# Attention's longer steps: two groups of key transpositions ahead of the scores, the column-tiled products ahead of the transpositions of probabilities

## What is computed

```python
q, k, v = att_qkv(rmsnorm(yp, norm_mix[l]), w_in_att[i], q_norm_g[i], k_norm_g[i])   # prompt, 16 heads of 64
res = [dilated_band(q, k, v, d, w // d) for (w, d) in PATTERNS]       # scores, exp, weighted sum of v
o = combine_patterns([r[0] for r in res], [r[1] for r in res])
...
kall = jnp.concatenate([cache_k[i].astype(jnp.float32), kn], axis=1)  # samples: 2048 cached keys each
vall = jnp.concatenate([cache_v[i].astype(jnp.float32), vn], axis=1)
res = [dilated_gather(qs, kall, vall, d, w // d) for (w, d) in PATTERNS]
```

## Time and profile before

| what | value |
|---|---|
| median of 3 runs | 2765.56 us (2764.55 to 2767.07) |
| time of the profiled execution | 2767.65 us |
| its span | 2765.8 us, 1.85 us less than its time |
| TensorE (PE) busy | 2714.1 us, 98% |
| VectorE (DVE) busy | 1741.2 us, 63% |
| ScalarE (ACT) busy | 947.4 us, 34% |
| attention | about 1497.5 to 1910 us from the span's start |

### The profile page before, as it was taken

The page is one execution under the profiler, slowest core; times in us unless marked ns, Lnnn a source line. Parts: engine busy times, 40 slices in busy tenths (PEclk is TensorE's granted clock), DMA queues, the critical chain, the costliest instruction groups (busy, mean ns, idle before and its releaser), DMA issues.

```text
span 2765.8 us, 56498 instructions
## 1 busy us (share of the span) xinstructions
PE 2714.1 (98%) x24481; PEld 2606.5 (94%) x24481; DVE 1741.2 (63%) x2867; ACT 947.4 (34%) x1697; POOL 97.4 (4%) x220
## 2 busy tenths in 40 slices
PE   7999999999999999999999999999999999999998
PEld 7998999999999999999998777777999999999998
DVE  5754536777677777765612666657377677766676
ACT  5543523322222222432224555554232222222222
POOL 1010000000000000000011111100000000000000
PEclk9999999999999999999999999999999999999999
DMA  5120120011111111133356777863101111111112
GB/s 201 36 81 14 61 102 31 31 48 61 47 47 46 47 47 46 60 129 95 95 177 218 252 254 240 273 224 130 58 16 47 46 47 47 47 47 47 58 50 81
DMA packets 126388, 254.64 MB, mean 92 GB/s; under 512 B 7617, under 2 KB 88725, under 8 KB 125632
## 3 DMA queue, kind: packets, MB, share of 16 engines
q1 hardware_dynamic: 112944, 189.26, 20.9%
q0 software_dynamic: 11888, 57.25, 6.0%
q10 hardware_dynamic: 1312, 4.52, 0.5%
HBM read 222.98 MB, written 28.02 MB: 91 GB/s over the span
## 4 chain that ended last, share of the span: by engine, by line
PE 92%; DVE 4%; ACT 2%; DMA 1%; issue 1%; POOL 0%; SPq 0%; ACTq 0%; DVEq 0%; POOLq 0%
PE psum L1574 30%; PE psum L1629 18%; PE psum L483 14%; PE psum L224 11%; PE psum L1549 3%; PE psum L2536 2%; PE psum L2492 2%; PE psum L2452 2%; PE psum L2477 2%; PE psum L2505 1%; PE psum L2557 1%; DVE att_scores L2710 1%; PE psum L592 1%; PE psum L2481 1%; ACT smp_kt L2592 0%
## 5 line engine op out<-in xcount | busy, mean ns | idle before, releaser
L1810 DVE TENSOR_TENSOR x_res<-x_res,psum 128x544 f32<-128x544 f32 x352 | 250.4, 719 | 154.8 <-PE psum L1629 154.6
L483 PE MATMUL psum<-w_hi,h_hi 128*128 128x256 f32 x1096 | 311.5, 284 | 1.0 <-ACT qkv_tok L2092 1.0
L483 PE MATMUL psum<-w_hi,h_lo 128*128 128x256 f32 x1096 | 307.9, 281 | 0.0
L483 PE MATMUL psum<-w_lo,h_hi 128*128 128x256 f32 x1096 | 307.3, 280 | 0.0
L1629 PE MATMUL psum<-ffn_hi,ffn_unit_hi 128*128 128x272 f32 x1408 | 292.6, 289 | 1.8 <-DVE x_res L1810 1.6
L1629 PE MATMUL psum<-ffn_lo,ffn_unit_hi 128*128 128x272 f32 x1408 | 291.5, 288 | 0.0
L1629 PE MATMUL psum<-ffn_hi,ffn_unit_lo 128*128 128x272 f32 x1408 | 290.7, 288 | 0.0
L1574 PE MATMUL psum<-h_hi,ffn_unit_lo 128*128 128x272 f32 x1280 | 265.2, 288 | 0.0
L1574 PE MATMUL psum<-h_lo,ffn_unit_hi 128*128 128x272 f32 x1280 | 264.8, 288 | 0.0
L1574 PE MATMUL psum<-h_hi,ffn_unit_hi 128*128 128x272 f32 x1280 | 264.5, 288 | 0.0
L1629 PEld LDWEIGHTS psum<-ffn_hi,ffn_unit_hi 128*128 128x128 f32 x1408 | 220.7, 188 | 3.2 <-DVE x_res L1810 3.2
(11 more groups left out here) (394 smaller groups left out, 5316.7 us busy)
## 6 DMA issues: line engine op xcount, KB each, us to landing
cache_tile<-in_cache_k SPq DMA_DIRECT2D x64, 512.0 KB, 8.0
cache_tile<-in_cache_v SPq DMA_DIRECT2D x64, 512.0 KB, 13.0
w_raw<-in_w_ffn_gate SPq DMA_DIRECT2D x22, 1024.0 KB, 5.1
w_raw<-in_w_ffn_up SPq DMA_DIRECT2D x22, 1024.0 KB, 5.1
w_raw<-in_w_ffn_down SPq DMA_DIRECT2D x22, 1024.0 KB, 4.8
w_raw<-in_w_in_att SPq DMA_DIRECT2D x12, 1024.0 KB, 7.1
w_raw<-in_w_in_rec SPq DMA_DIRECT2D x10, 1024.0 KB, 4.9
park_x<-x_res POOLq DMA_DIRECT2D x2, 4368.0 KB, 13.3
```

What stands on the lines that cost most here:

```text
L483: mm = pe.matmul(PS[0:n, bank, 0:BW], st[:, k, w:w + n], mv[slot][:, k * BW:(k + 1) * BW], start=(k == 0 and x == 0) if used is None else ...
L1810: dve.tensor_tensor(x, x, pset(dset(g, i)), ALU.add).then_inc(s_res, 1)
```

## The change

In a long step (`keys_lead`) PE runs key groups 0 and 1, then the scores, then key groups 2 and 3, then at the end of phase 2 the weighted values and the sample products, and only then the turns of probabilities. ScalarE copies all four key groups before the first exponential, and VectorE takes the sample products before the probabilities' copies. The banks of the turns, their count, all shapes and all waits' values stay. Steps other than the 28 keep their order.

```diff
-    SCORED = {(0, 3): (0, 1), (1, 3): (2, 3), (2, 3): (4, 5), (3, 3): (6, 7), (4, 3): (8, 9)}
-    PV_AT = {0: 3, 1: 3, 2: 3, 3: 3, 4: 3}
+    def keys_lead(n):
+
+        return 0 <= n < NSLOT and n % QT >= 4 and sample_slot(n)[1] in (1, 2, 3, 4)
+
+    def scored(n, f):
+
+        s = sample_slot(n)[1]
+        return (2 * s, 2 * s + 1) if s is not None and s < 5 and f == (2 if keys_lead(n) else 3) else ()
+
+    def weighed_at(n):
+
+        s = sample_slot(n)[1]
+        return 1 if s is None or s > 4 else 2 if keys_lead(n) else 3
...
             b, s = sample_slot(n)
-            if 0 <= n < NSLOT and f == 1:
+            if 0 <= n < NSLOT and f == 1 and not keys_lead(n):
                 scores(n)
             for i in phase(n, f):
                 turn(n, i)
-            if 2 <= n and f == PV_AT.get(s, 1):
+            if f == 1 and keys_lead(n):
+                scores(n)
+            if 2 <= n and f == weighed_at(n):
                 pv(n - 2)
-            for t in SCORED.get((s, f), ()):
+            for t in scored(n, f):
                 tile_scores(b, t)
...
             mine = [i for i, u in enumerate(turns(n)) if by_act(u)]
-            for i in mine[0:2]:
+            first = 4 if keys_lead(n) else 2
+            for i in mine[0:first]:
                 take_act(act, n, i)
             if 0 <= n < NSLOT:
                 probs(n, 0)
-            for i in mine[2:4]:
+            for i in mine[first:4]:
                 take_act(act, n, i)
...
-                for t in SCORED.get((s, f), ()):
+                for t in scored(n, f):
                     if t % 2:
                         piece(b, t // 2)
```

## The result

The changed kernel is slower by about 3 us: 2768.52 us in the median of 22 runs (2764.97 to 2776.26) against 2765.53 (2763.81 to 2768.33, 22 runs), a ratio of 1.0012 with a 95% interval of 1.0006 to 1.0017.

What follows compares the result with a forecast made beforehand. The prediction took TensorE, 92% of 2765.8 us, as the bound; 17.1 us saved less 2.4 for shape changes and 14.6 for new VectorE waits left 0.1 us, so 2765.5 us, range 2760 to 2773.

Steps and rivals of the forecast that it cites:

- What it saves: In long steps, third and fourth key groups' delay behind ScalarE and block 7's wait for the reduction go: 17.1 us.
- Changes of shape: Blocks 4 to 7 gain a net two array-shape changes a pair of heads, at 0.17 us each: 2.4 us added.
- rival 2: The new shape change from key turns to scores costs 0.41 us in all 28 long steps: 2772.2 us, chance 0.07.
- The run of turns: New waits on VectorE's copies: 0.90 in block 6, 0.95 in block 7, 0.23 in block 0; 14.6 us added.
- Rival 1: VectorE empties the banks in time, so the 14.6 us of new waits are absent: 2750.9 us, chance 0.13.
- ScalarE: Copying all four key groups before its exponentials, ScalarE still serves the sample products in time, 0.35 us to spare.
- rival 3: ScalarE falls behind, and third key group or sample products wait again: up to 2780.6 us, chance 0.06.
- Key tiles: The key group behind the scores is asked for about 1.2 us sooner; some 5 us is to spare.
- rival 4: Key tiles arrive late for the key group now asked for sooner: a few us slower, say 2770, chance 0.04.
- Sum: Over the seven pairs, 17.1 - 2.4 - 14.6 = 0.1 us saved, against the profiled execution's 2767.65 us.

Runs made afterwards that it cites:

- thin loads: Only a quarter of each cache tile's columns loaded and used four times: 2753.68 us on the changed kernel, 2755.36 us on the kernel before.
- second batch: The changed kernel measured again with no edit, for a second profile: 2767.25 us in 11 runs, ratio 1.0005.
- limit of four loads: At most four cache-tile loads under way, added to the changed kernel with four banks for the first two key groups: 2754.86 us, ratio 0.9962.
- four banks: Changed kernel with all four banks open to the first two key groups of its 28 long steps: 2762.22 us, ratio 0.9987.
- The shift: Changed kernel with 128 more waits on TensorE at the program's start, moving its later instructions: 2774.88 us, ratio 1.0038.

## Why the prediction was wrong

*What it saves*: right. The third group's 28 waits on ScalarE and block 7's on the reduction are gone. *Changes of shape*: right, 0.17 from key turns to scores (1847.69); rival 2 is out. *The run of turns*: right to 0.05 us; 0.90 and 0.95 were worked out, 0.85 and 0.91 stand there, and the steps moved as forecast (blocks 4 and 5 shorter by 0.44 and 0.53, 6 and 7 longer by 0.31 and 0.29, block 0 by 0.20, in the stretch without stops). Rival 1 (banks free in time) is out. *ScalarE*: right; in attention its copies hold the sample products up once, for 0.4 us, so rival 3 is out. *Key tiles*: on PE's side a load of keys is named once in the changed kernel's two traces, for 0.2 us, so rival 4 is out. *Sum*: 0.1 us saved; the regular time says 1.3 (0.18 a pair), the thin loads 0.8 in the pairs, so the terms were a little too dear. Up to here the mechanism was right.

The step that failed is the one behind the sum: "17.1 - 2.4 - 14.6 = 0.1 us saved, against the profiled execution's 2767.65 us". It takes all time outside the terms as fixed. 10.4 us of the kernel before (2765.8 less the 2755.4 of its thin version) and 13.6 to 14.8 of the changed one were stops and delays beside full cache loads. What they are shows when a trace is laid against that of its thin version, weight load by weight load. The kernel before loses 12.3 us there: 4.8 at the 197th to 199th places, 3.8 at the start of attention, 0.8 at the last pair's value tile, the rest in small pieces, with the granted clock at 0.50 behind two of the delays. The 3.8 begin with this wait, behind which VectorE's row names a transfer, `out_v_sample<-qkv_tok`:

```profile
1505.74 0.85 PEld L2481 LDWEIGHTS psum<-ident,att_k 128*128 128x128 f32 x8 [2.71 <-DVE smp_pt L2674]
```

The changed kernel's second trace loses 14.0: 7.3 at such places, 3.8 and 0.8 at the same two others. Its first trace loses 22.7, with 8.7 at such places and more stretches at the lower clock. So what differs is the stops for want of instructions, 4.8 us before and 7.3 and 8.7 after. By the medians, the change is 1.7 us faster with thin loads and 3.0 slower with full ones, 4.7 in all, or 3.1 with the second batch; up to 1.0 of it can be the late tile of keys in the thin version of the kernel before. The prediction read "issue" as change of shape everywhere, named no supply of instructions among the bounds, and its first part, "TensorE shows 28.04 us of matmul but only 23.19 us of weight loads", was read at a DMA share of 1.02 without asking what else needs the DMA engines. The time lies in the stated range, but the kernel got slower, not 0.1 us faster.

What stays open: why exactly these blocks stop, since each fetch's delay depends on the loads around it, why the stops grew with the change in place of shrinking, and how much of the 4.7 us would remain with other blocks at other places. Nor was the limit of four loads tried without the four banks. The shift gave about the same (some 2770 against 2767 to 2769), which speaks against a lucky or unlucky alignment alone.

## What to carry to other kernels

Where TensorE runs short instructions while loads fill the DMA engines, look for idle time "issue" inside a run of equal instructions, and set it against the packets of the instruction queue; if they come late, a wait removed may be paid back there. Ask PE's side as well as PEld's before calling idle time "issue": here PE's row named a load where PEld's did not. Holding the loads back by their number under way is worth a try: two made tiles late, four gave 7 us here. And a scatter of some us between runs of one kernel can be a sign: here it went with the bytes of the cache loads.

## What the runs showed of the hardware

- TensorE's instructions came in 196 packets of 16.4 KB. A packet took 0.9 to 1.5 us; in quiet stretches it started 0.60 to 0.98 blocks past its block's start, beside cache loads up to 1.75, and then TensorE stood for up to 2.7 us, always at the 197th to 199th instruction of a block by my count, and went on 1.3 to 1.6 us behind the packet's end.
- Behind stops of 2.22 and 2.67 us, and in the shifted kernel behind one of 1.75, the granted clock fell to 0.50, 1.2 GHz; behind one of 1.95 us it stayed at 1.00.
- Two waits of the program for one semaphore became one instruction: 128 waits added 64 records.
- With a quarter of the cache's bytes the same instructions ran within 0.9 us from lowest to highest, with all of them within 4.5 (before) and 11.3 (after), though in 22 runs against 5.
